# Second pair's input rows fetched with the late operands, and expert retrieval in seven pieces behind seven steps, in a hybrid decoder layer

## The chip, the cores and the metric

The kernel runs on one core of one Trainium2 chip. The metric is the device time of one execution in microseconds (us), all transfers from and to HBM included.

## The reference

One layer of a decoder runs over 512 prompt tokens and 8 x 4 sample tokens, width 1024, all in float32. First comes a mixer (projections, a causal convolution of width 31, dilated attention with 24 heads, gates, an output projection), then the part with which most of this text deals, a mixture of 16,384 one-neuron experts:

```python
def peer_block(hb):                                   # hb: normalised rows
    q = (hb @ w_peer_q).reshape(rows, 8, 2, 128)
    s = jnp.einsum('thpc,hpkc->thpk', q, sub_keys)    # two halves, 128 keys each
    s1, i1 = lax.top_k(s[:, :, 0], 16)
    s2, i2 = lax.top_k(s[:, :, 1], 16)
    cand = (s1[..., :, None] + s2[..., None, :]).reshape(rows, 8, 256)
    top_s, top_c = lax.top_k(cand, 16)
    idx = take(i1, top_c // 16) * 128 + take(i2, top_c % 16)
    g = softmax(top_s)
    a = jnp.einsum('td,tkd->tk', hb, expert_u[idx])
    return jnp.einsum('tk,tkd->td', g * gelu(a), expert_v[idx])
```

## The kernel before

**Tiles and pairs.** The prompt's four tiles of 128 rows are 0, 1, 2 and 3, the 32 sample rows are tile 4. `PAIRS` puts tiles 0, 1 and 4 through the mixer first and tiles 2 and 3 second. `plan()` writes the mixer out as 508 ticks of tasks; each engine's program walks the same ticks in order (`TICKS`), and semaphores alone join the engines. SP issues all plain transfers in this order, POOL the gathers.

**Steps.** The experts are worked off in 544 steps (`ST`). A step gathers 128 rows of 8 KB (one expert's `u` and `v` row for each partition, 1.05 MB) into one of the `RING` = 6 slots of the tile `ring` (POOL, L1106, an indirect transfer). DVE takes the dot product of the `u` half with the token's row in `rep` (L1945), ACT makes `gelu` and a folding matrix of it (L1514, L1518, L1521), PE adds the weighted `v` half up in `acc` (L1348) and counts `v_used`; with that count POOL may issue the gather that takes the slot next, six steps on. Steps 0 to 127 belong to tile 0, 128 to 255 to tile 1, 256 to 287 to tile 4, then 128 each to tiles 2 and 3. `MARK` says after which tick how many steps are done: 272 of them run among the ticks of the second pair's mixer, the last 272 alone behind it. The loop is the function `steps_upto` of each engine.

**Items.** Each tile has 8 heads, and each (tile, head) is an item of `ITEMS`: 40 in all. An item with 128 rows serves 16 steps, one of tile 4 serves 4. Its retrieval on DVE finds the 16 best of both halves of 128 scores, the 16 best of the 256 sums, and the experts' numbers and weights. `item_list` lets the retrieval of an item for 16 steps begin 16 steps before its first one; tile 4's items lie between these, at steps 8, 40, 72 and so on. `part(q, p)` is piece p of item q, and `PARTS` puts piece p behind the dot product of step at + p. Then PE spreads the result over the partitions (`spread`, L1310), DVE copies it to `pick` (`place`, L1903 and L1904), and POOL and ACT wait on `pick_ready` before the first step of the item. `place_picks` chooses the tick of spread and place, or in the last 272 steps the step at + 5 (`TAIL_PICKS`), where `place` comes two steps later on DVE. The first pair's scores go through HBM: SP fetches those of the next item (`load_scores`, at the step in `SCORES_AT`) when `half_done` says that the last one's halves are searched. ACT makes the exponentials (`head_exp`, L1503).

**Input rows.** `xt` holds two tiles of x in the tile `sx`, which the attention's scores use as well. The task `X0` of a tile waits on ACT for its rows (`x_in`), squares them (L1556), then POOL and DVE scale them and PE turns them (`XT`). For tiles 2 and 3 `X0` stands in the ticks of the first pair's query projection (`wq`), and SP fetches the rows in that same tick. `ENDS["late", 0]` is an earlier tick, at which the first pair's attention is over (`o_free`); there SP fetches operands of the first pair's end: x for the residual, norm weights, taps, sub keys (`skT`).

**Copies on the chip.** For tiles 2 and 3 the rows in `rep` are made on PE (`copy_rows`) and copied out by ACT.

Of the kernel before, what the change touches and what calls it, by code (L numbers as in the profile page):

```python
# [9 lines left out]
ALU = mybir.AluOpType  # L10
# [3 lines left out]
P = 128  # L14
# [18 lines left out]
LOW = -3.0e38  # L33
# [63 lines left out]
def tile_rows(t):  # L97
    return P if t < NT else SMP
# [104 lines left out]
LEAD_V, LEAD_A = 2, 2  # L203
# [244 lines left out]

ITEMS = item_list()
ITEM_NO = {(t, h): q for q, (_, t, h) in enumerate(ITEMS)}  # L450
PARTS = {}
for _q, (_at, _t, _h) in enumerate(ITEMS):
    for _p in range(4):
        if _at >= 0:
            PARTS.setdefault(_at + _p, []).append((_q, _p))
SCORES_AT = {ITEMS[q - 1][0] + 2 if q > 2 and (t, h) != (2, 0) else max(at - 3, 0): q for q, (at, t, h) in enumerate(ITEMS) if at >= 0}


def place_picks():

    tail = {}
    for q, (at, _, _) in enumerate(ITEMS):
        n = START if q == 0 else next((n for n in range(START, len(TICKS)) if MARK[n] + LEAD_V > at + 3), len(TICKS)) + 2
        if n < len(TICKS):
            TICKS[n].append(("P", q))
            TICKS[n].sort(key=lambda v: ORDER[v[0]])
        else:
            tail[at + 5] = q  # L470
    return tail


# [136 lines left out]
def program(nc, a, sc):  # L610
    with ExitStack() as ctx:
# [176 lines left out]
        def o_phase(p):  # L788
            return max(OB.no["O", x] for x in XS if PH_OF[pair(x)[0]] == p) + 1
# [29 lines left out]
        def _(eng):  # L819
# [110 lines left out]
            for n, tick in enumerate(TICKS):  # L930
# [7 lines left out]
                for p in range(2):  # L938
                    if n == ENDS["late", p]:
                        eng.wait_ge(o_free, o_phase(p))  # L940
                        for j in range(2):
                            eng.wait_ge(v_out[j], out_last(V_OUT, p, 2 + j))
                            if p == 0:
                                eng.wait_ge(hist_out[j], out_last(HIST, p, 2 + j))
                        for t in PAIRS[p][0:2]:
                            eng.dma_start(x1s[:, t % 2, :], a["x_prompt"][0, P * t:P * (t + 1), :]).then_inc(late_in, 16)
                        eng.dma_start(w2, a["norm2_w"].to_broadcast([P, D])).then_inc(late_in, 16)
                        if p == 0:
                            eng.dma_start(pt[:, D:D + 2 * P], a["taps"]).then_inc(taps_in, 16)
                            for j in range(2):  # L950
                                eng.wait_ge(ub_out[j], max(UB_OUT[i] for i, (t, _) in enumerate(GLU) if i % 2 == j and PH_OF[t] == 0))
                            for c in range(2):
                                load_last_u(c)
                        eng.dma_start(skT, a["sk_t"]).then_inc(late_in, 16)
                if n == ENDS["cp", NT, 1]:
                    eng.wait_ge(conv_v, DC * TAPS)
                    for c in range(QUAD):
                        row = slice(SUB * c, SUB * (c + 1))
                        eng.dma_start(x1d[row, :].rearrange("p (h x) -> p h x", h=2), xs.rearrange("t (h c x) -> t c h x", h=2, c=QUAD)[:, c]).then_inc(dlate_in, 16)
                        eng.dma_start(w2d[row, :].rearrange("p (h x) -> p h x", h=2),  # L960
                                      a["norm2_w"].rearrange("o (h c x) -> o c h x", h=2, c=QUAD)[:, c].to_broadcast([SUB, 2, P])).then_inc(dlate_in, 16)
                for v in tick:
                    if v[0] == "X0" and v[1] in (2, 3):
                        t = v[1]
                        eng.wait_ge(o_free, o_phase(0))
                        eng.dma_start(xt[:, t % 2, :], a["x_prompt"][0, P * t:P * (t + 1), :]).then_inc(x_in[t % 2], 16)
                    elif v[0] == "uo":
                        t, c = v[1:]
                        i = NTH["G", t, c]
                        freed(eng, ZB, z_free, ("glu", t, c))  # L970
# [528 lines left out]
        def _(eng):  # L1499
# [7 lines left out]
            def steps_upto(last):  # L1507
                for i in range(done[0], min(last, STEPS)):
                    t, h, j, s = ST[i]
                    if j == J_ORDER[t][0] and s == 0:  # L1510
                        eng.wait_ge(pick_ready, ITEM_NO[t, h] + 1)
                    if i >= 2:
                        eng.wait_ge(fold_ready, i - 1)
                    eng.activation(by_pick[:, i % 2, :], cst[:, C_FOLD:C_FOLD + SUB], ACT.Copy, scale=picks(i, 1)).then_inc(by_ready, 1)  # L1514
                    eng.wait_ge(dot_ready, i + 1)
                    if i >= 4:
                        eng.wait_ge(v_used, i - 3)
                    eng.activation(gel[:, i % 4:i % 4 + 1], dots[:, i % 4:i % 4 + 1], ACT.Gelu).then_inc(gel_ready, 1)  # L1518
                    eng.wait_ge(gel_ready, i + 1)
                    eng.wait_ge(by_ready, i + 1)  # L1520
                    eng.activation(fold[:, i % 4, :], by_pick[:, i % 2, :], ACT.Copy, scale=gel[:, i % 4:i % 4 + 1]).then_inc(fold_ready, 1)  # L1521
                    for n, u, k in MADE.get(i, ()):
                        eng.wait_ge(rep_made, n + 1)
                        eng.wait_ge(dot_ready, slot_before(u, k) + 1)
                        for w in range(2):
                            ins = eng.activation(rep[:, k, 512 * w:512 * (w + 1)], zb[w][:, :], ACT.Copy)
                        ins.then_inc(rep_ready, 1)
                    for q, p in PARTS.get(i, ()):
                        if p == 1:
                            head_exp(q)  # L1530
                done[0] = max(done[0], last)

# [263 lines left out]
        def _(eng):  # L1796
# [40 lines left out]
            def top16(values, index, x):  # L1837
                link(eng.max(values[:, 0:8], x))
                link(eng.max_index(index[:, 0:8], values[:, 0:8], x))  # L1839
                link(eng.match_replace(x, values[:, 0:8], x, LOW))  # L1840
                link(eng.max(values[:, 8:16], x))  # L1841
                return eng.max_index(index[:, 8:16], values[:, 8:16], x)  # L1842

            def halves(q):
                _, t, h = ITEMS[q]
                m, of = tile_rows(t), sco2
                if PH_OF[t]:
                    freed(eng, SB, s_free, ("SC", t, h // 2))
                    of = kept_scores(t)[:, 2 * KEYS * h:2 * KEYS * (h + 1)]
                elif q:  # L1850
                    eng.wait_ge(sco_in, 16 * q)
                else:
                    freed(eng, SB, s_free, ("SC", 0, 0))
                    link(eng.tensor_copy(sco2[:, :], sco[:, 0, 0:2 * KEYS]))
                for p in range(2):
                    ins = top16(tv[0:m, p, :], ti[0:m, p, :], of[0:m, KEYS * p:KEYS * (p + 1)])
                    if p:
                        signal(ins, half_done, q + 1)
                    else:
                        link(ins)  # L1860

            def candidates(q):
                m = tile_rows(ITEMS[q][1])
                link(eng.tensor_copy(tif[0:m, :, :], ti[0:m, :, :]))
                if q:
                    eng.wait_ge(o_ready, OB.no["P", q - 1] + 1)
                link(eng.tensor_tensor(cand[0:m, :, :], tv[0:m, 0, :].unsqueeze(2).to_broadcast([m, TOPK, TOPK]),
                                       tv[0:m, 1, :].unsqueeze(1).to_broadcast([m, TOPK, TOPK]), ALU.add))
                link(top16(cv[0:m, :], ci[0:m, :], cand[0:m, :, :].rearrange("p a b -> p (a b)")))
                signal(eng.tensor_scalar(nmx[0:m, :], cv[0:m, 0:1], -1.0, None, ALU.mult), top_ready, q + 1)  # L1870

            def keys_named(q, p):
                m = tile_rows(ITEMS[q][1])
# [8 lines left out]

            def experts(q):
                m = tile_rows(ITEMS[q][1])
                keys_named(q, 1)
# [19 lines left out]
                eng.sem_inc(o_free, 1)  # L1905

            def part(q, p):
                if p == 0:
                    halves(q)
                elif p == 1:  # L1910
                    candidates(q)
                elif p == 2:
                    keys_named(q, 0)
                else:
                    experts(q)

# [37 lines left out]
            for n, tick in enumerate(TICKS):  # L1954
# [182 lines left out]
                if n in CONV[0]:  # L2137
                    conv_upto(0, CONV[0][n])
                if START - 4 <= n < START:
                    part(0, n - START + 4)  # L2140
# [68 lines left out]
```

## Time and profile before

| | us |
|---|---|
| median of 3 runs | 2246.28 |
| lowest and highest run | 2244.76, 2247.51 |
| profiled execution, its own time | 2251.89 |
| span of the profiled execution | 2250.1 |
| DVE busy | 1469.5 (65%) |
| PE busy | 1631.4 (73%) |
| ACT busy, POOL busy | 867.5 (39%), 751.8 (33%) |
| bytes moved, mean rate | 745.18 MB, 331 GB/s |

The span runs from the first to the last instruction of the profiled execution, which took 5.61 us longer than the median of the three plain runs. All rows below are of that execution, so differences are worked out against 2251.89. A busy share is a mean over stages with different limits: up to about 530 us there are no expert steps, to about 1560 us steps and mixer run together, and behind that the steps run alone.

### The profile page before, as it was taken

To read this page: it belongs to the slowest core of one execution; us is meant where nothing else is said; L and a number is where in the kernel's file an instruction comes from. 1 tells how busy PE (TensorE), PEld (TensorE's weight loads), DVE (VectorE), ACT (ScalarE), POOL (GpSimd) and SP (SyncE) were. 2 spreads that over 40 slices of the span, in tenths; PEclk is the share of its full clock that TensorE was granted. 3 is DMA by queue.
4 is the path that set the end of the run, shared out by engine and by line. 5 is a ranking of instruction groups with operands and counts; after the bars stand their busy time and mean duration, and the time that the engine had idled before them with its cause. 6 is when DMAs were issued, how large, how long until landed. Compare 5 with 4: busy or idle time off the path is not lost.

```text
span 2250.1 us, 33792 instructions
## 1 busy us (share of the span) xinstructions
PE 1631.4 (73%) x11740; PEld 748.3 (33%) x11740; DVE 1469.5 (65%) x3591; ACT 867.5 (39%) x2442; POOL 751.8 (33%) x713
## 2 busy tenths in 40 slices
PE   7999999997898977777778989996444344444343
PEld 3556655443443433434343433342100001100000
DVE  2577764114658687878877767446766766766764
ACT  2122334012445434544546653334333333333332
POOL 1254200001332344333442323334444344344343
PEclk9999999998999989789888999997655556555555
DMA  5333556666898979899989999999999999999998
GB/s 192 130 110 110 200 217 237 251 201 259 324 400 339 378 302 374 303 374 364 383 332 381 362 397 405 380 406 401 389 387 412 411 406 408 389 404 399 391 386 354
DMA packets 125798, 745.18 MB, mean 331 GB/s; under 512 B 15892, under 2 KB 39052, under 8 KB 47916
## 3 DMA queue, kind: packets, MB, share of 16 engines
q0 software_dynamic: 78336, 570.46, 63.9%
q1 hardware_dynamic: 47292, 172.55, 20.6%
q8 instruction: 94, 1.54, 0.3%
q14 instruction: 76, 0.62, 0.1%
HBM read 727.36 MB, written 16.44 MB: 331 GB/s over the span
## 4 chain that ended last, share of the span: by engine, by line
PE 36%; DMA 25%; DVE 24%; issue 9%; ACT 4%; POOL 2%; SPq 0%; DVEq 0%; POOLq 0%; ACTq 0%
DMA ring<-in_expert_uv,pick 23%; PE z L1174 21%; DVE ring L1945 5%; PE acc L1348 5%; PE z L1180 2%; DMA sx<-in_x_prompt 1%; PE o L1209 1%; DVE ti L1839 1%; DVE ti L1842 1%; DVE cand L1880 1%; DVE e L1881 1%; DVE tv L1841 1%; DVE cand L1878 1%; DVE tmp L2016 1%; PE s L1478 1%
## 5 line engine op out<-in xcount | busy, mean ns | idle before, releaser
L1106 POOL DMA_INDIRECT ring<-in_expert_uv,pick x544 | 619.7, 1139 | 949.5 <-PE acc L1348 859.4
L1945 DVE CUSTOM_DVE_ANT_0 ring<-ring,rep 128x1024 f32<-128x1024 f32 x544 | 660.1, 1225 | 351.1 <-DMA ring<-in_expert_uv,pick 318.4
L1348 PE MATMUL acc<-ring,fold 128*32 128x256 f32 x4352 | 452.0, 506 | 456.0 <-ACT fold L1521 454.2
L1174 PE MATMUL z<-wts,hT 128*128 128x384 f32 (+1 forms) x1408 | 613.6, 573 | 7.6 <-ACT hT L1536 4.7
L1518 ACT ACTIVATE gel<-dots 128x1 f32<-128x1 f32 x544 | 109.9, 202 | 727.3 <-DVE dots L1945 723.6
L1348 PEld LDWEIGHTS acc<-ring,fold 128*32 128x32 f32 x4352 | 106.3, 124 | 767.2 <-ACT fold L1521 687.5
L1174 PEld LDWEIGHTS z<-wts,hT 128*128 128x128 f32 x1408 | 260.4, 199 | 259.8 <-issue 197.6
L1174 PE MATMUL z<-wts,yT 128*128 128x512 f32 x384 | 194.6, 643 | 10.9 <-ACT yT L1717 5.9
L1521 ACT ACTIVATE fold<-by_pick,gel 128x32 f32<-128x32 f32 x544 | 175.6, 323 | 18.0
L1514 ACT ACTIVATE by_pick<-cst,pick 128x32 f32<-128x32 f32 x544 | 168.1, 309 | 0.0
L1831 DVE SCALAR_TENSOR_TENSOR yT<-uT,vec,yT 128x256 f32<-128x256 f32 x240 | 107.8, 501 | 2.3
L1174 PEld LDWEIGHTS z<-wts,yT 128*128 128x128 f32 x384 | 71.5, 201 | 99.5 <-issue 99.4
L1071 POOL TENSOR_SCALAR xss<-xss 128x1 f32<-128x1 f32 (+1 forms) x10 | 2.0, 196 | 275.6 <-ACT kvr L1732 218.3
L1518 ACT ACT_TABLE_LOAD x70 | 89.8, 1283 | 1.2
L1071 POOL TENSOR_SCALAR ssq<-ssq 128x6 f32<-128x6 f32 (+1 forms) x40 | 21.6, 539 | 179.8 <-DVE ssq L2000 179.0
L1209 PE MATMUL o<-kvr,pt 128*128 128x64 f32 x432 | 59.1, 294 | 13.2 <-ACT pt L1536 10.3
L1402 PE MATMUL t<-cst,sx 128*128 128x128 f32 x216 | 39.6, 304 | 39.8 <-ACT hoT L1536 22.9
L1209 PEld LDWEIGHTS o<-kvr,pt 128*128 128x128 f32 x432 | 58.4, 211 | 23.8 <-ACT pt L1536 13.4
L2032 DVE SCALAR_TENSOR_TENSOR sx<-s,cst 128x512 f32<-128x512 f32 (+3 forms) x72 | 36.8, 552 | 39.6 <-PE s L1199 37.5
L1072 POOL TENSOR_TENSOR ssq<-ssq,half_m 128x6 f32<-128x6 f32 (+1 forms) x40 | 53.4, 1336 | 3.5 <-POOL ssq L1071 0.2
L1672 ACT ACTIVATE sx<-sx,nm 128x384 f32<-128x384 f32 (+3 forms) x32 | 32.5, 1017 | 56.6 <-DVE nm L2043 56.3
L1536 ACT ACTIVATE pt<-t 128x512 f32<-128x512 f32 (+2 forms) x64 | 33.6, 524 | 51.4 <-PE t L1402 51.3
(256 smaller groups left out, 1760.9 us busy)
## 6 DMA issues: line engine op xcount, KB each, us to landing
wts<-in_w_qkv SPq DMA_DIRECT2D x24, 1536.0 KB, 7.9
wts<-in_w_glu SPq DMA_DIRECT2D x8, 2048.0 KB, 9.8
wts<-in_w_gate SPq DMA_DIRECT2D x8, 2048.0 KB, 12.3
wts<-in_w_wq SPq DMA_DIRECT2D x8, 2048.0 KB, 10.7
ring<-in_k_cache SPq DMA_DIRECT2D x16, 768.0 KB, 7.3
ring<-in_v_cache SPq DMA_DIRECT2D x16, 768.0 KB, 7.0
ring<-in_expert_uv,pick POOLq DMA_INDIRECT x544, 10.8
wts<-in_w_cp SPq DMA_DIRECT2D x4, 2048.0 KB, 10.5
```

The costliest lines, as they stand in the source:

```text
L1072: return eng.tensor_tensor(to, to, half_m[0:m, 0:w], ALU.pow)
L1106: eng.indirect_dma_start(ring[:, i % RING, :], None, a["expert_uv"], bass.IndirectOffsetOnAxis(picks(i, 0).bitcast(U32), 0)).then_inc(row_ ...
L1174: mm = eng.matmul(bank[:, 0:w], of[:, k, :], rows[:, k, :], start=(k == 0), stop=(k == depth - 1))
L1180: mm = eng.matmul(to, of[:, k, :], by, start=(k == 0), stop=(k == depth - 1))
L1209: mm = eng.matmul(ob[:, 0:HD], pt[:, P * j:P * (j + 1)], vv[:, hp % 2, u, P * g + HD * w:P * g + HD * (w + 1)], start=(j == 0), stop=(j == ...
L1348: mm = eng.matmul(acc[b][SUB * c:SUB * (c + 1), col:col + 256], fold[:, i % 4, :], ring[:, i % RING, D + 256 * c:D + 256 * (c + 1)], start ...
L1402: mm = eng.transpose(tpb[:, P * (j - 4 * q):P * (j - 4 * q + 1)], s_sb[:, XN[x] % 2, P * j:P * (j + 1)], ident)
L1514: eng.activation(by_pick[:, i % 2, :], cst[:, C_FOLD:C_FOLD + SUB], ACT.Copy, scale=picks(i, 1)).then_inc(by_ready, 1)
L1518: eng.activation(gel[:, i % 4:i % 4 + 1], dots[:, i % 4:i % 4 + 1], ACT.Gelu).then_inc(gel_ready, 1)
L1521: eng.activation(fold[:, i % 4, :], by_pick[:, i % 2, :], ACT.Copy, scale=gel[:, i % 4:i % 4 + 1]).then_inc(fold_ready, 1)
L1831: ins = eng.scalar_tensor_tensor(out=out, in0=src, scalar=cw[:, c, tap:tap + 1], in1=out, op0=ALU.mult, op1=ALU.add)
L1945: eng.tensor_tensor_reduce(u, u, rep[:, j, :], 1.0, 0.0, ALU.mult, ALU.add, dots[:, i % 4:i % 4 + 1]).then_inc(dot_ready, 1)
```

## The change

It has two parts. SP fetches the rows of tiles 2 and 3 at the tick `ENDS["late", 0]`, as the last transfers of that group, and no longer at their `X0`. And the retrieval of an item is cut in seven pieces behind seven steps where it had four behind four: each half search alone, the sums with the first eight of their best, the second eight, each of the two key lookups alone, the experts' numbers. The operations are the same, and so is their order within an item. What hangs on the end of a retrieval moves along: `spread` and `place` come three steps later, `head_exp` is put behind step at + 4 where it was behind step at + 1, and the next item's scores are fetched one step later. Item 0's pieces stay in the same four ticks.

```diff
+PIECES = 7
 PARTS = {}
 for _q, (_at, _t, _h) in enumerate(ITEMS):
-    for _p in range(4):
+    for _p in range(PIECES):
         if _at >= 0:
             PARTS.setdefault(_at + _p, []).append((_q, _p))
-SCORES_AT = {ITEMS[q - 1][0] + 2 if q > 2 and (t, h) != (2, 0) else max(at - 3, 0): q for q, (at, t, h) in enumerate(ITEMS) if at >= 0}
+SCORES_AT = {ITEMS[q - 1][0] + 3 if q > 2 and (t, h) != (2, 0) else max(at - 3, 0): q for q, (at, t, h) in enumerate(ITEMS) if at >= 0}
...
-        n = START if q == 0 else next((n for n in range(START, len(TICKS)) if MARK[n] + LEAD_V > at + 3), len(TICKS)) + 2
+        n = START if q == 0 else next((n for n in range(START, len(TICKS)) if MARK[n] + LEAD_V > at + PIECES - 1), len(TICKS)) + 2
...
-            tail[at + 5] = q
+            tail[at + PIECES + 1] = q
...
                         eng.dma_start(skT, a["sk_t"]).then_inc(late_in, 16)
+                        if p == 0:
+                            for t in PAIRS[1]:
+                                eng.dma_start(xt[:, t % 2, :], a["x_prompt"][0, P * t:P * (t + 1), :]).then_inc(x_in[t % 2], 16)
...
-                    if v[0] == "X0" and v[1] in (2, 3):
-                        t = v[1]
-                        eng.wait_ge(o_free, o_phase(0))
-                        eng.dma_start(xt[:, t % 2, :], a["x_prompt"][0, P * t:P * (t + 1), :]).then_inc(x_in[t % 2], 16)
...
-                        if p == 1:
+                        if p == 4:
                             head_exp(q)
...
             def part(q, p):
-                if p == 0:
-                    halves(q)
-                elif p == 1:
-                    candidates(q)
-                elif p == 2:
-                    keys_named(q, 0)
+                if p < 2:
+                    half_search(q, p)
+                elif p < 4:
+                    candidates(q, p - 2)
+                elif p < 6:
+                    keys_named(q, p - 4)
                 else:
                     experts(q)
```

On SP the two fetches of x into `sx` stood directly behind a weight load that waits for PE (`z_ready`), in the ticks of the query projection, among the scores that go out to HBM (`x_sc`) and come back (`sco`):

```order
L827 DMA wts<-in_w_wq 128x4096 [waits z_ready]
L966 DMA sx<-in_x_prompt 128x1024 [waits o_free]
L1032 DMA x_sc<-tmp 128x512 [waits s_free_a]
L857 DMA sco<-x_sc 32x256 [waits sco_out0,half_done]
L1032 DMA x_sc<-tmp 32x512 [waits s_free_a]
L1032 DMA x_sc<-tmp 128x512 [waits s_free_a]
L827 DMA wts<-in_w_glu 128x4096 [waits z_ready]
L966 DMA sx<-in_x_prompt 128x1024 [waits o_free]
```

Now they stand as one group behind the sub keys (`kvr<-in_sk_t`), ahead of the next part of the sample tokens' value cache, which is read into the tile `ring` before the gathers use it:

```order
L849 DMA qTs<-x_uh 32x256 [waits ub_out1,ub_out0]
L849 DMA qTs<-x_uh 32x256
L955 DMA kvr<-in_sk_t 128x2048
L958 DMA sx<-in_x_prompt 128x1024 x2
L842 DMA ring<-in_v_cache 128x1536 [waits k_used]
L842 DMA ring<-in_v_cache 128x1536 x3
L828 DMA wts<-in_w_ap 128x2048 [waits z_ready]
```

Both fetches have moved past all weight loads of the output and query projections and past the first fetches of scores.

On DVE, behind the dot product (ISA; its line is 1945 before, 1957 in the changed kernel) of the first step of the last item, both half searches stood together, each of five operations, and the next step's dot product behind ten:

```order
L1945 ISA dots 128x1
L1838 MAX tv<-uT 128x8
L1839 MAX_INDEX ti<-tv,uT 128x8
L1840 MATCH_REPLACE uT<-tv,uT 128x128
L1841 MAX tv<-uT 128x8
L1842 MAX_INDEX ti<-tv,uT 128x8
L1838 MAX tv<-uT 128x8
L1839 MAX_INDEX ti<-tv,uT 128x8
L1840 MATCH_REPLACE uT<-tv,uT 128x128
L1841 MAX tv<-uT 128x8
L1842 MAX_INDEX ti<-tv,uT 128x8
L1945 ISA ring,dots<-ring,rep 128x1024
```

Now the next step's dot product stands behind five, and the second half behind that:

```order
L1957 ISA dots 128x1
L1838 MAX tv<-uT 128x8
L1839 MAX_INDEX ti<-tv,uT 128x8
L1840 MATCH_REPLACE uT<-tv,uT 128x128
L1841 MAX tv<-uT 128x8
L1842 MAX_INDEX ti<-tv,uT 128x8
L1957 ISA ring,dots<-ring,rep 128x1024
L1957 ISA dots 128x1
L1838 MAX tv<-uT 128x8
L1839 MAX_INDEX ti<-tv,uT 128x8
L1840 MATCH_REPLACE uT<-tv,uT 128x128
L1841 MAX tv<-uT 128x8
```

The second half search has moved behind one more dot product; the later pieces follow in the same way, one behind each of the next five.

## Rows read from the trace of the kernel before

**Rows 1.** The page's chain that ended last, by line.

```profile
DMA ring<-in_expert_uv,pick 23%; PE z L1174 21%; DVE ring L1945 5%; PE acc L1348 5%; PE z L1180 2%; DMA sx<-in_x_prompt 1%; PE o L1209 1%; DVE ti L1839 1%; DVE ti L1842 1%; DVE cand L1880 1%; DVE e L1881 1%; DVE tv L1841 1%; DVE cand L1878 1%; DVE tmp L2016 1%; PE s L1478 1%
```

**Rows 2.** By stage: busy us (instructions) of PE, PEld, DVE, ACT, POOL; PEclk, DMA share, GB/s.

```profile
500.00:620.00 120.00, 91.63 (x613) 47.19 (x615) 63.18 (x199) 43.30 (x121) 26.34 (x26) 0.89 0.79 290
...
900.00:1220.00 320.00, 244.05 (x1501) 126.59 (x1499) 267.37 (x695) 169.92 (x418) 120.10 (x106) 0.87 0.94 358
...
1600.00:2000.00 400.00, 171.55 (x1388) 38.60 (x1388) 283.71 (x708) 143.62 (x499) 179.26 (x154) 0.55 0.99 403
```

**Rows 3.** The chain, 480 to 660 us: start, length, what.

```profile
540.33 11.44 DMA sx<-in_x_prompt
...
581.16 14.90 DMA sx<-in_x_prompt
```

**Rows 4.** Waits, 500 to 620 us: total, times, longest.

```profile
ACT pt L1556 <- DMA sx<-in_x_prompt: 24.0, 2, 12.7
```

**Rows 5.** Timeline of PE, 520 to 612 us; in brackets the idle time before.

```profile
555.73 1.08 PE L1348 MATMUL acc<-ring,fold 128*32 128x256 f32 x8 [12.62 <-ACT fold L1521]
...
597.94 0.47 PE L1466 MATMUL t<-cst,uT 128*128 128x128 f32 x1 [10.30 <-ACT hoT L1536]
```

**Rows 6.** Timeline of SP's issues, 380 to 640 us.

```profile
415.62 2.26 SPq L841 DMA_DIRECT2D ring<-in_v_cache  x4
```

**Rows 7.** The chain, 380 to 460 us.

```profile
416.96 9.46 DMA ring<-in_v_cache
```

**Rows 8.** Timeline of DVE, 2033 to 2052 us.

```profile
2034.04 1.22 DVE L1945 CUSTOM_DVE_ANT_0 ring<-ring,rep 128x1024 f32<-128x1024 f32 x1 [1.25 <-DMA ring<-in_expert_uv,pick]
...
2037.03 0.29 DVE L1838 MAX8 tv<-uT 128x8 f32<-128x128 f32 x1
...
2038.87 1.22 DVE L1945 CUSTOM_DVE_ANT_0 ring<-ring,rep 128x1024 f32<-128x1024 f32 x1
...
2041.69 0.09 DVE L1840 MATCH_VALUE_LOAD cand<-cv,cand 128x8 f32 x1
...
2043.39 1.22 DVE L1945 CUSTOM_DVE_ANT_0 ring<-ring,rep 128x1024 f32<-128x1024 f32 x1
...
2046.54 1.23 DVE L1945 CUSTOM_DVE_ANT_0 ring<-ring,rep 128x1024 f32<-128x1024 f32 x1
...
2049.05 0.17 DVE L1886 SCALAR_TENSOR_TENSOR e<-e 128x16 f32<-128x16 f32 x1
...
2050.09 1.23 DVE L1945 CUSTOM_DVE_ANT_0 ring<-ring,rep 128x1024 f32<-128x1024 f32 x1
...
2051.24 1.22 DVE L1945 CUSTOM_DVE_ANT_0 ring<-ring,rep 128x1024 f32<-128x1024 f32 x1
```

**Rows 9.** Busy time in stretches of 2 us.

```profile
2044.00:2046.00 2.00, 0.07 (x4) 0.07 (x8) 1.86 (x7) 1.94 (x5) 0.00 (x0) 0.50 1.01 422
...
2048.00:2050.00 2.00, 1.08 (x8) 0.20 (x8) 1.79 (x7) 0.55 (x3) 0.77 (x2) 0.50 0.64 160
```

**Rows 10.** Timeline of POOL's gather issues, 2036 to 2062 us.

```profile
2042.13 0.94 POOL L1106 DMA_INDIRECT ring<-in_expert_uv,pick  x1 [3.90 <-PE acc L1348]
...
2047.31 1.26 POOL L1106 DMA_INDIRECT ring<-in_expert_uv,pick  x1 [4.24 <-PE acc L1348]
```

**Rows 11.** The chain, 2034 to 2064 us.

```profile
2051.36 0.21 ACT gel L1518
...
2051.97 1.12 PE acc L1348 x8
```

**Rows 12.** Timeline of DVE: the dot products of steps 272, 528 and 540.

```profile
1528.10 1.23 DVE L1945 CUSTOM_DVE_ANT_0 ring<-ring,rep 128x1024 f32<-128x1024 f32 x1 [1.26 <-DMA ring<-in_expert_uv,pick]
...
2204.18 1.23 DVE L1945 CUSTOM_DVE_ANT_0 ring<-ring,rep 128x1024 f32<-128x1024 f32 x1 [1.25 <-DMA ring<-in_expert_uv,pick]
...
2234.35 1.23 DVE L1945 CUSTOM_DVE_ANT_0 ring<-ring,rep 128x1024 f32<-128x1024 f32 x1 [1.25 <-DMA ring<-in_expert_uv,pick]
```

**Rows 13.** Waits, whole span.

```profile
DVE pick L1903 <- PE o L1310: 29.7, 11, 7.3
```

More of the change, by code:

```diff
@@ L962, in _ @@
                 for v in tick:
-                    if v[0] == "X0" and v[1] in (2, 3):
-                        t = v[1]
-                        eng.wait_ge(o_free, o_phase(0))
-                        eng.dma_start(xt[:, t % 2, :], a["x_prompt"][0, P * t:P * (t + 1), :]).then_inc(x_in[t % 2], 16)
-                    elif v[0] == "uo":
+                    if v[0] == "uo":
                         t, c = v[1:]
@@ L1842, in top16, with scores_of @@
                 return eng.max_index(index[:, 8:16], values[:, 8:16], x)
-            def halves(q):
+            def scores_of(q, p):
                 _, t, h = ITEMS[q]
                 m, of = tile_rows(t), sco2
+                if p:
+                    return m, kept_scores(t)[:, 2 * KEYS * h:2 * KEYS * (h + 1)] if PH_OF[t] else of
                 if PH_OF[t]:
@@ L1854, in halves, with half_search, candidates @@
                     link(eng.tensor_copy(sco2[:, :], sco[:, 0, 0:2 * KEYS]))
[L1855 to L1862, printed above, removed]
-                m = tile_rows(ITEMS[q][1])
+                return m, of
+            def half_search(q, p):
+                m, of = scores_of(q, p)
+                ins = top16(tv[0:m, p, :], ti[0:m, p, :], of[0:m, KEYS * p:KEYS * (p + 1)])
+                if p:
+                    signal(ins, half_done, q + 1)
+                else:
+                    link(ins)
+            def candidates(q, p):
+                m = tile_rows(ITEMS[q][1])
+                flat = cand[0:m, :, :].rearrange("p a b -> p (a b)")
+                if p:
+                    link(eng.match_replace(flat, cv[0:m, 0:8], flat, LOW))
+                    link(eng.max(cv[0:m, 8:16], flat))
+                    link(eng.max_index(ci[0:m, 8:16], cv[0:m, 8:16], flat))
+                    signal(eng.tensor_scalar(nmx[0:m, :], cv[0:m, 0:1], -1.0, None, ALU.mult), top_ready, q + 1)
+                    return
                 link(eng.tensor_copy(tif[0:m, :, :], ti[0:m, :, :]))
@@ L1868, in candidates @@
                                        tv[0:m, 1, :].unsqueeze(1).to_broadcast([m, TOPK, TOPK]), ALU.add))
-                link(top16(cv[0:m, :], ci[0:m, :], cand[0:m, :, :].rearrange("p a b -> p (a b)")))
-                signal(eng.tensor_scalar(nmx[0:m, :], cv[0:m, 0:1], -1.0, None, ALU.mult), top_ready, q + 1)
+                link(eng.max(cv[0:m, 0:8], flat))
+                link(eng.max_index(ci[0:m, 0:8], cv[0:m, 0:8], flat))
             def keys_named(q, p):
@@ L1884, in experts @@
                 m = tile_rows(ITEMS[q][1])
-                keys_named(q, 1)
                 link(eng.scalar_tensor_tensor(out=e12[0:m, 0, :], in0=e12[0:m, 0, :], scalar=float(KEYS), in1=e12[0:m, 1, :], op0=ALU.mult, op1=ALU.add))
@@ L2139, in _ @@
                 if START - 4 <= n < START:
-                    part(0, n - START + 4)
+                    k = 2 * (n - START + 4)
+                    for p in range(k, min(k + 2, PIECES)):
+                        part(0, p)
                 steps_upto(lead(n, LEAD_V))
```

## The prediction

> **What bounds the kernel now.** I read the page's chain first: the kernel has no single bound. Of the work that ended last, 23% is gathers of expert rows, 21% the mixer's matrix products, and 1% is a transfer of x [rows 1]. So I went by stages. In the stage from 900 to 1220 us DVE is busy 267 of 320 us, PE 244, and the transfer engines 94%: three engines near their limit that wait for one another. From 1600 to 2000 us only expert steps run, PE is busy 43%, DVE 71% and the transfer engines 99%, with 403 GB/s [rows 2]. There the gathers are the bound, and the question is whether they run without holes.
>
> The fetch of x is seen in the chain: 11.44 us from 540.33 and 14.90 us from 581.16 [rows 3]. ACT stands still for them 24.0 us in two waits [rows 4], and PE behind ACT twice, 12.62 us before 555.73 and 10.30 us before 597.94 [rows 5].
>
> The retrieval is seen in DVE's timeline of one item near 2034 us [rows 8]. Dot products start at 2034.04, 2038.87, 2043.39, 2046.54 and 2050.09, and the next at 2051.24, so that one with nothing behind it takes 1.15 us. Without retrieval the last period's steps 528 to 540 go from 2204.18 to 2234.35, 2.514 us a step [rows 12]; this is the pace of the gathers. The four pieces make 16.05 us of four steps that were due in 10.06: DVE ends 6.0 us late.
>
> What the lateness does is seen two steps on. A gather takes the slot that a step six before it gives free. The dot product of 2038.87 is 2.32 us late against the pace; the gather it releases goes out at 2042.13, and between 2044 and 2046 us the transfers still run at 422 GB/s. The dot product of 2043.39 is 4.32 us late; its gather goes out at 2047.31, and between 2048 and 2050 the rate is 160 GB/s [rows 9, 10]. So a lateness of 2.3 us is covered by the queue, one of 4.3 us is not.
>
> **The tail: 272 steps alone.** Step 272 starts at 1528.10 and step 528 at 2204.18 [rows 12]: 676.08 us for 256 steps, 2.641 us a step or 42.25 us for 16. At 2.514 it would be 40.22. The difference is 2.03 us an item, and 16 items are searched there (at steps 272 to 512, every 16): 32.5 us.
>
> Would seven pieces close the holes? The pieces come out of [rows 8]: a half search 1.84 us (2035.19, which is 2034.04 and 1.15, to 2037.03, and again to 2038.87), the sums with the first eight 1.67 (2040.02 to 2041.69), the second eight 1.70, the first lookup 2.00, the second 1.36, the experts' numbers 1.04; in all 11.45. A step takes 1.15 and its piece. Against 2.514 DVE's lateness then goes 0.48, 0.95, 1.26, 1.59, 2.23, 2.23, 1.90 us and falls off by 1.36 a step. Its peak of 2.23 lies just below the 2.32 that left no hole. I take the whole 32 us. Above it, with every step at the 422 GB/s of [rows 9], a step takes 2.485 us and the gain is 16 x 16 x 0.156 = 40 us; below, it is nothing, if the holes have another cause (a rival).
>
> ACT's exponential moves three steps later and its waits on DVE with it. Its operations are the same and it is needed only by the last piece, two steps on; I count 0.
>
> **The input rows.** Both fetches go out with the sub keys, before 415.62 us, where SP issues the next part of the value cache [rows 6], over 120 us before ACT wants them. ACT's waits vanish. PE loses 22.9 us in its two stalls, of which I leave 2 for work of ACT that still lies between (in the first stall PE resumes 3.96 us after the rows have landed at 551.77). So 21. But the transfers of this stage must then go into a shorter time: 290 GB/s over 120 us [rows 2] are 34.8 MB; less 1.05 MB of x they need 341 GB/s over 99 us. That is below 403 and so can be done, yet gathers and weights will now and then stand in each other's way; I give 4 us back (bounds 0 and 10). At their new place the fetches are 1.05 MB ahead of the value cache, which is on the chain with 9.46 us [rows 7]: 2.6 us at 403 GB/s if the queue is full then, 0 if it has run dry; I take 2, since the transfers ahead of it were issued in one group. Net 15 us, between 10 and 23.
>
> The rows show why x was slow: 0.52 MB took 11.44 and 14.90 us [rows 3], though at 403 GB/s they need 1.3; they went out right behind a weight load. The Trainium skill (DMA: Bandwidth & Descriptors, Issuing engines are not separate DMA queues) says that transfers from all issuing engines run on the same 16 engines and interleave; the trace agrees. By that rule the early fetch gets nothing for free and pays the upper bound at the value cache, which would make the sum smaller by 0.6 us.
>
> **The middle: 272 steps among the second pair's ticks.** 23 items are searched there. DVE does ticks and pieces in one line, so a long piece holds up mixer tasks on which PE waits, and the ring has holes as in the tail. If each item gave 2.03 us as in the tail, this were 47 us; if PE and the order of the ticks set the pace alone, 0. As three engines share the bound [rows 2], I take a quarter, 12 us, an estimate.
>
> The waits that are moved: `place` stands three steps later, at + 10. POOL may issue the gather of step at + 16 when PE has counted step at + 10. PE's products for a step end 1.85 us behind its dot product (2051.24 to 2053.09) [rows 8, 11], and `place` is two small copies, at most 0.74 us by the mean 0.37 of the five operations of a half search. So the picks come about 1.1 us before they can be used, where they came three steps before. Cost 0 here; what is queued behind a late `place` is all of DVE and POOL's gathers (a rival). SP fetches scores one step later; the next item begins at least 5 steps on, some 12 us or more even at the tail's pace. Cost 0.
>
> **Sum.** 32 + 15 + 12 = 59. The profiled execution took 2251.89 us and would take 2193. The median of the runs is 5.61 us below the profiled execution, so I predict 2187.
>
> **The rivals.**
>
> The gathers keep their mean pace whatever DVE does: the holes are made up by the bursts behind them, and 42.25 us for 16 is what memory gives. For it: at 403 GB/s the tail is near its best short stretches. Against it: 160 GB/s right where a gather was late [rows 9, 10], and 2.514 us over 12 steps without an item. Then tail and middle give nothing and x alone gives 15: 2231. The Trainium skill (DMA: Bandwidth & Descriptors, Specifications) gives about 358 GB/s as the limit of HBM for a core. By it a step could not be under 2.93 us and the tail would have nothing to give; the trace disagrees, with 403 over 400 us and 422 in a short stretch [rows 2, 9].
>
> The time that x gives is lost again: the gathers and weights behind 540 us take as long as before, and the stall comes back as a wait of DVE on the ring. For it: the stage's transfer engines are busy 79% with the stalls in it. Against it: 341 GB/s are below what the tail moves. Then the gain is 44: 2202.
>
> Slower: `place` becomes the thing that gathers wait for. DVE waits there for PE's `spread`, 29.7 us in 11 of the 40 places now, at most 7.3 [rows 13], and the margin shrinks from three steps to 1.1 us. If `place` is late by w on the other 39 items, this costs 39 x (w - 1.1); from w = 2.6 us the gain of 59 is gone. At 4 us each it costs 113: 2300. Against it: PE spreads two steps ahead of `place`, and the searches end four steps ahead.
>
> The change does not act: DVE is late by as much in the end (the same 11.45 us), ACT or the ticks set the pace: 2246.
>
> **How the numbers follow.** Forecast 0.63; mean pace kept 0.18; x lost again 0.10; `place` late 0.06; no effect 0.03. The likeliest is 2187. With the upper bounds of tail and x and 30 for the middle the gain is 93: 2153. Upwards the range takes in the second rival and goes halfway into the first's, to 2226, which leaves out about 2 in 10. The likeliest case's own range is 2153 to 2205. A measurement of this kernel tells some 0.2% (4.5 us) from no change. Faster 0.91, within 0.2% 0.03, slower 0.06.
>
> **What would show it.** Tail: 16 steps in 40 to 40.5 us, no 2 us stretch below 300 GB/s behind an item, dot products of an item some 3 us apart. Input rows: no wait of ACT on x behind 500 us, and PE without the two stalls; the value cache's piece of the chain up to 2 us longer. Middle: step 272 some 27 us earlier than 1528. I am wrong if holes stay though DVE is less than 2.5 us late, or if POOL waits for `pick`.

## The result, and the profile after

The changed kernel takes 2190.74 us, the median of 4 runs (2186.95 to 2192.8); the kernel before, on the same chip, 2245.52 (4 runs, 2237.85 to 2247.51). The ratio is 0.9754 with an interval of 0.9737 to 0.9771. The forecast was 2187. The profiled execution took 2191.63 us with a span of 2189.8.

The page's chain that ended last, by line, which answers to [rows 1]:

```profile
DMA ring<-in_expert_uv,pick 25%; PE z L1174 20%; DVE ring L1957 9%; PE acc L1348 4%; PE z L1180 2%; PE o L1209 1%; DVE ti L1839 1%; DVE tmp L2028 1%; DVE ti L1842 1%; DVE nm L2054 1%; DVE tmp L2021 1%; POOL ring L1106 1%; PE s L1199 1%; ACT fold L1521 1%; DVE tv L1841 1%
```

The transfer of x is gone from it. Gathers (25%) and dot products (9%, before 5%) hold more of a shorter time.

By stage, columns as in [rows 2]:

```profile
500.00:620.00 120.00, 111.48 (x782) 57.55 (x781) 71.42 (x218) 54.06 (x151) 32.53 (x34) 0.97 0.92 351
900.00:1220.00 320.00, 256.35 (x1577) 130.19 (x1574) 265.88 (x675) 181.69 (x443) 128.37 (x110) 0.88 0.96 371
1600.00:2000.00 400.00, 179.87 (x1444) 39.95 (x1444) 294.55 (x733) 149.65 (x522) 206.70 (x159) 0.53 1.01 418
```

Between 500 and 620 us PE is busy 111 us instead of 92, and the transfers run at 351 GB/s instead of 290. In the tail they run at 418 instead of 403. In the middle DVE is busy as long as before, and 1577 matrix products fit where 1501 did.

DVE's timeline of one item in the tail, dot products alone, which answers to [rows 8], and those of steps 272 and 528, which answer to [rows 12]:

```profile
1495.04 1.23 DVE L1957 CUSTOM_DVE_ANT_0 ring<-ring,rep 128x1024 f32<-128x1024 f32 x1 [1.26 <-DMA ring<-in_expert_uv,pick]
...
1983.42 1.23 DVE L1957 CUSTOM_DVE_ANT_0 ring<-ring,rep 128x1024 f32<-128x1024 f32 x1 [1.25 <-DMA ring<-in_expert_uv,pick]
1986.41 1.23 DVE L1957 CUSTOM_DVE_ANT_0 ring<-ring,rep 128x1024 f32<-128x1024 f32 x1
1989.39 1.23 DVE L1957 CUSTOM_DVE_ANT_0 ring<-ring,rep 128x1024 f32<-128x1024 f32 x1
...
1995.06 1.23 DVE L1957 CUSTOM_DVE_ANT_0 ring<-ring,rep 128x1024 f32<-128x1024 f32 x1
1998.21 1.23 DVE L1957 CUSTOM_DVE_ANT_0 ring<-ring,rep 128x1024 f32<-128x1024 f32 x1
...
2004.08 1.22 DVE L1957 CUSTOM_DVE_ANT_0 ring<-ring,rep 128x1024 f32<-128x1024 f32 x1
...
2145.16 1.23 DVE L1957 CUSTOM_DVE_ANT_0 ring<-ring,rep 128x1024 f32<-128x1024 f32 x1 [1.25 <-DMA ring<-in_expert_uv,pick]
```

The starts of an item's steps now stand 2.8 to 3.2 us apart instead of up to 4.8. From 1495.04 to 2145.16 are 650.1 us for 256 steps, 40.63 us for 16 (before 42.25).

POOL's gathers behind that item, and the transfers in stretches of 2 us at the same place; the views are those of [rows 10] and [rows 9]:

```profile
1989.67 1.76 POOL L1106 DMA_INDIRECT ring<-in_expert_uv,pick  x1 [1.23 <-PE acc L1348]
...
1998.32 1.93 POOL L1106 DMA_INDIRECT ring<-in_expert_uv,pick  x1 [1.23 <-PE acc L1348]
2002.11 0.94 POOL L1106 DMA_INDIRECT ring<-in_expert_uv,pick  x1 [1.86 <-PE acc L1348]
```

```profile
1996.00:1998.00 2.00, 1.06 (x8) 0.20 (x8) 1.83 (x8) 1.62 (x3) 1.10 (x1) 0.50 1.01 422
1998.00:2000.00 2.00, 0.02 (x3) 0.00 (x0) 1.93 (x5) 1.97 (x5) 1.68 (x1) 0.50 1.02 422
2000.00:2002.00 2.00, 1.08 (x8) 0.20 (x8) 1.93 (x5) 0.85 (x4) 0.25 (x1) 0.50 1.01 401
2002.00:2004.00 2.00, 1.08 (x8) 0.20 (x8) 1.86 (x5) 0.74 (x3) 0.94 (x2) 0.50 1.01 410
```

The gathers still go out unevenly (3.79 us from 1998.32 to 2002.11), but the rate stays at 401 and above where it fell to 160 before.

At the start the value cache holds the mixer up for longer than in [rows 7]. The chain of the changed kernel, and then PE's timeline there:

```profile
416.92 11.56 DMA ring<-in_v_cache
```

```profile
428.61 5.92 PE L1262 MATMUL o<-ring,rep 128*32 128x512 f32 x32 [4.26 <-DMA ring<-in_v_cache]
...
549.33 0.64 PE L1348 MATMUL acc<-ring,fold 128*32 128x256 f32 x8 [1.96 <-ACT fold L1521]
```

The transfer takes 2.1 us more than the 9.46 before. The 32 products behind it begin at 428.61 (before 426.56) and take 5.92 us (before 3.64). The last line is the place of the stall of 12.62 us in [rows 5]: 1.96 are left. Nothing answers to the second stall, or to ACT's wait on x in [rows 4].

### The profile page after: what moved, and what is told of

It is laid out like the page before. It is cut to its first block, busy times and chain, and to the rows that moved or that the text cites. A ratio compares the mean times of both kernels' runs of the same rounds, so it can differ in the third digit from the quotient of the medians.

```text
span 2189.8 us, 33814 instructions
## 1 busy us (share of the span) xinstructions
PE 1623.5 (74%) x11740; PEld 742.6 (34%) x11740; DVE 1466.1 (67%) x3591; ACT 865.0 (40%) x2442; POOL 796.4 (36%) x713
## 4 chain that ended last, share of the span: by engine, by line
PE 35%; DMA 26%; DVE 25%; issue 8%; ACT 5%; POOL 2%; SPq 0%; DVEq 0%; ACTq 0%; POOLq 0%
DMA ring<-in_expert_uv,pick 25%; PE z L1174 20%; DVE ring L1957 9%; PE acc L1348 4%; PE z L1180 2%; PE o L1209 1%; DVE ti L1839 1%; DVE tmp L2028 1%; DVE ti L1842 1%; DVE nm L2054 1%; DVE tmp L2021 1%; POOL ring L1106 1%; PE s L1199 1%; ACT fold L1521 1%; DVE tv L1841 1%
## 5 line engine op out<-in xcount | busy, mean ns | idle before, releaser
L1106 POOL DMA_INDIRECT ring<-in_expert_uv,pick x544 | 665.4, 1223 | 876.5 <-PE acc L1348 804.9
L1174 PE MATMUL z<-wts,yT 128*128 128x512 f32 x384 | 188.1, 625 | 13.2 <-ACT yT L1717 8.6
L1672 ACT ACTIVATE sx<-sx,nm 128x384 f32<-128x384 f32 (+3 forms) x32 | 32.5, 1016 | 51.5 <-DVE nm L2055 51.2
## 6 DMA issues: line engine op xcount, KB each, us to landing
ring<-in_expert_uv,pick POOLq DMA_INDIRECT x544, 11.3
```

The lines of the kernel that those rows point to most:

```text
L1106: eng.indirect_dma_start(ring[:, i % RING, :], None, a["expert_uv"], bass.IndirectOffsetOnAxis(picks(i, 0).bitcast(U32), 0)).then_inc(row_ ...
L1174: mm = eng.matmul(bank[:, 0:w], of[:, k, :], rows[:, k, :], start=(k == 0), stop=(k == depth - 1))
```

## The experiments

All runs in one table, from the trace of one execution each: the starts of the dot products of steps 0, 16, 272 and 528, and us for 16 steps in the middle (16 to 272) and in the tail (272 to 528). The last column is the median of the plain times; "(one)" marks a single run.

```
              step 0  step 16 step 272 step 528  middle  tail   median of times
before         531.0   607.9   1528.1   2204.2   57.51  42.26   2245.52
after          535.3   594.6   1495.0   2145.2   56.28  40.63   2190.74
after_again    536.6   593.4   1495.6   2145.6   56.39  40.62   2190.37
after_third    534.4   594.1   1493.7   2143.8   56.23  40.63   2189.45
x_only         534.1   592.4   1507.8   2178.6   57.21  41.92   2226.57
pieces_only    534.8   617.0   1514.1   2164.5   56.07  40.65   2210.05
tail_pieces    535.8   595.8   1512.8   2162.4   57.31  40.60   2207.48
x_behind       531.2   589.7   1489.6   2141.4   56.25  40.73   2188.87
x_sk_behind    530.5   588.0   1484.8   2135.1   56.05  40.65   2184.76
x_sk_second    530.9   589.0   1485.5   2134.7   56.03  40.58   2181.98
spaced4        535.9   592.9   1499.6   2152.0   56.67  40.78   2200.22
late_place     536.6   592.9   1493.2   2143.6   56.27  40.65   2190.18 (one)
ring5_after    536.8   595.7   1537.8   2208.9   58.88  41.94   2255.36 (one)
ring5_before   532.5   611.8   1581.5   2288.8   60.61  44.21   2335.47 (one)
```

### Each half of the change alone: x_only, pieces_only, tail_pieces, after_again

The theory is the forecast's: tail, input rows and middle are three gains of their own. The first rival says that the gathers keep their mean pace and only x counts; the second, that x's time is lost again behind 540 us.

x_only is the kernel before, with the early fetch alone:

```diff
                         eng.dma_start(skT, a["sk_t"]).then_inc(late_in, 16)
+                        if p == 0:
+                            for t in PAIRS[1]:
+                                eng.dma_start(xt[:, t % 2, :], ...).then_inc(x_in[t % 2], 16)
...
-                    if v[0] == "X0" and v[1] in (2, 3):
-                        t = v[1]
-                        eng.wait_ge(o_free, o_phase(0))
-                        eng.dma_start(xt[:, t % 2, :], ...).then_inc(x_in[t % 2], 16)
-                    elif v[0] == "uo":
+                    if v[0] == "uo":
```

> Early fetch of x alone, retrieval in four pieces as before. My theory: the two ACT waits on x go and PE's stalls with them, less some 4 us because the value cache lands later; step 16 starts near 595 us and the median is 13 us below before, near 2232 us. Rival, that the stage's transfers take the time back: within 4 us of before, 2242 to 2250 us.

pieces_only is the changed kernel with this diff turned round, so that x comes late as before.

> Seven pieces alone, x fetched late as before. My theory: the tail gains 26 us (40.6 us for 16 steps), the middle some 17, so near 2203 us, and the gains of this and of the early fetch alone add up to the 55 us of both. Rival, that the gathers keep their mean pace: tail at 42.2 us for 16 steps and a median above 2235 us.

tail_pieces has the early fetch, and seven steps for a retrieval only where it starts at step 272 or behind; the earlier items are done behind four steps, in the groups of before:

```diff
+def behind(q):
+    return (0, 1, 2, 3, 4, 5, 6) if ITEMS[q][0] >= BASE[2] - LAG else (0, 0, 1, 1, 2, 3, 3)
...
-            PARTS.setdefault(_at + _p, []).append((_q, _p))
+            PARTS.setdefault(_at + behind(_q)[_p], []).append((_q, _p))
...
-            tail[at + PIECES + 1] = q
+            tail[at + behind(q)[-1] + 2] = q
```

For those earlier items ACT's exponential goes back to the step behind `at`, and the next item's scores are fetched one step earlier again, for all items.

> Early x, seven pieces in the last 272 steps alone, four pieces for the items before. My theory, that tail and middle gain each by itself: tail at 40.6 us for 16 steps, 17 us slower than the changed kernel, near 2207 us. Rival, that pieces help in the tail alone and the earlier step 272 is due to x: as the changed kernel, 2191 us.

after_again is the changed kernel on this chip.

> The changed kernel once more, beside the others on the same chip: 2187 to 2193 us by every theory.

Measured, with the kernel before at 2243.89 on this chip: x_only 2226.57 (ratio 0.9922, 0.9896 to 0.9948), pieces_only 2210.05 (0.9846, 0.9823 to 0.9869), tail_pieces 2207.48 (0.9832, 0.9806 to 0.9859), after_again 2190.37 (0.9756, 0.9733 to 0.978). The halves add: 17.3 and 33.8 are 51.2, and both together give 53.5. So x's time isn't lost again, and the pieces act without it. tail_pieces has the tail of the changed kernel (40.60) and the middle of x_only (57.31 against 57.21). It ends 17.1 us above after_again: that is the middle's share. x_only in turn ends 19.1 us above tail_pieces: that is the tail's. So by the medians the change consists of 17.3 us for x, 19.1 for the tail and 17.1 for the middle.

x_only did better than its forecast of 2232; pieces_only missed its own, near 2203, by 7 us. Its tail is the expected 40.65 and its middle 56.07, but step 16 comes 9.1 us later than in the trace of the kernel before. There ACT waits 28.8 us for x instead of 24.0; why x comes still later in this kernel isn't shown.

What the middle's share consists of is seen in the waits between 610 and 1490 us (total, times, longest). In tail_pieces:

```profile
DVE ring L1968 <- DMA ring<-in_expert_uv,pick: 117.6, 71, 7.4
POOL ssq L1083 <- DVE ssq L2023: 82.4, 16, 11.6
```

and in after_again:

```profile
DVE ring L1957 <- DMA ring<-in_expert_uv,pick: 110.7, 64, 6.2
POOL ssq L1071 <- DVE ssq L2012: 72.7, 16, 8.7
```

DVE waits 6.9 us less for gathers, and POOL 9.7 us less for DVE's sums of squares, a part of the mixer's norms. That both grow shorter fits the reason of the forecast (a long piece leaves holes in the ring and holds up the mixer's tasks). How the 17 us divide between the two isn't settled by it: waits of two engines may overlap.

### Where x goes out: x_behind, x_sk_behind, x_sk_second, after_third

After the first runs the value cache at the start was the one place where the change lost time. x_behind sends x behind the small operands that SP fetches after the value cache's last part, instead of ahead of it:

```diff
-                        if p == 0:
-                            for t in PAIRS[1]:
-                                eng.dma_start(xt[:, t % 2, :], ...).then_inc(x_in[t % 2], 16)
...
                                       ....to_broadcast([SUB, 2, P])).then_inc(dlate_in, 16)
+                    for t in PAIRS[1]:
+                        eng.dma_start(xt[:, t % 2, :], ...).then_inc(x_in[t % 2], 16)
```

> The changed kernel with x for tiles 2 and 3 fetched behind the sample's late operands, that is behind the value cache's second part, near 424 us. My theory: the value cache lands after 9.5 us again, PE's pause ahead of it is short and its clock stays up, step 0 starts at 531 us where it started at 535, and the median is 4 us below the changed kernel, near 2187 us. Rival, that the steps' transfers set the pace from 540 us on and hide the start: 2191 us.

x_sk_behind moves the sub keys of the first pair there too:

```diff
-                        eng.dma_start(skT, a["sk_t"]).then_inc(late_in, 16)
+                        if p:
+                            eng.dma_start(skT, a["sk_t"]).then_inc(late_in, 16)
...
+                    eng.dma_start(skT, a["sk_t"]).then_inc(late_in, 16)
                     for t in PAIRS[1]:
```

> As the one before, and the sub keys (1 MB) fetched there too. My theory: the value cache lands 2.6 us earlier still (1.05 MB at 403 GB/s), so about 6.5 us below the changed kernel, near 2184 us. Rival, as before: 2191 us.

Measured, with the kernel before at 2246.0: x_behind 2188.87 (0.9738, 0.9722 to 0.9754) and x_sk_behind 2184.76 (0.9727, 0.9708 to 0.9747). In both, step 0 stands where it stood in the kernel before. x_behind's median doesn't decide between 2187 and the rival's 2191, since the changed kernel didn't run beside it. The 2.6 us that the sub keys were to bring weren't there: the value cache lands at 425.7 us in x_sk_behind and at 426.7 in x_behind, and the times of the two overlap (2181.22 to 2190.58, 2185.06 to 2190.61). To set the better one beside the changed kernel itself, both ran once more on one chip (kernel before 2245.29), as x_sk_second and after_third.

> The changed kernel, the measure for the run beside it on the same chip: 2187 to 2193 us.

> x and the sub keys both fetched behind the value cache, once more and beside the changed kernel. My theory: step 0 near 531 us where the changed kernel has 535 to 537, and 4 to 7 us below it in time. Rival, that the gain seen was scatter between chips: within 2 us of it.

x_sk_second took 2181.98 (2181.22 to 2188.22; 0.9722, 0.9701 to 0.9743), after_third 2189.45 (2185.9 to 2195.23; 0.9747, 0.9724 to 0.977). The medians are 7.5 us apart, and the intervals of the ratios overlap. PE's timeline of x_sk_second shows where a part of the time comes from:

```profile
425.95 3.64 PE L1263 MATMUL o<-ring,rep 128*32 128x512 f32 x32 [1.47 <-DMA ring<-in_v_cache]
```

The products begin 2.7 us earlier than in the first profile of the changed kernel, and take 3.64 us instead of 5.92. Beside after_third, step 0 comes 3.5 us earlier, step 16 5.0, step 272 8.2 and step 528 9.1; what it gains behind step 16 has no cause that these runs show, and may be the scatter of single executions. This is the best version found.

### How much lateness the queue covers: spaced4, late_place, ring5_after, ring5_before

The forecast says that not the length of a piece matters but how late DVE is in sum against the pace of the gathers, and that the queue covers 2.3 us and not 4.3. spaced4 tells the two apart. The four long pieces are back, but each with an idle step behind it, so that an item still takes seven steps:

```diff
+def behind(q):
+    return (0, 0, 2, 2, 4, 6, 6)
```

with the uses of `behind` as in tail_pieces, and `place` where the changed kernel has it.

> The changed kernel with the four long pieces back, but behind every second step (at, + 2, + 4, + 6); place stands as in the changed kernel. By the lateness at 2.514 us a step: 2.3, 1.0, 3.0, 1.6, 2.2, 0.9, 1.9 us, a peak of 3.0. My theory, that the sum of lateness decides: between the 2.3 that left no hole and the 4.3 that did, 0 to 0.7 us an item, 2191 to 2202 us. Rival, that the length of one piece (3.7 us) decides: the tail at 42 us for 16 steps again, 2213 us or more.

Measured: 2200.22 (0.9793, 0.9772 to 0.9814). The tail takes 40.78 for 16 steps, near the changed kernel's 40.63 and far from 42.26. From the traces, the mean of 16 items: us from each of the first nine steps to the next.

```
before     4.83 4.54 3.15 3.54 1.22 1.15 1.15 1.80 1.85
after      3.02 2.99 2.82 2.85 3.23 2.52 2.18 1.19 1.93
spaced4    4.83 1.15 4.52 1.15 3.22 1.15 3.60 1.19 1.83
```

Against a pace of 2.486 (the steps behind 528 of the changed kernel's trace), the greatest lateness in sum is 6.1 us before, 2.5 after, and 3.0 in spaced4 (4.83, 1.15 and 4.52 less three times 2.486). A piece of 3.7 us does little harm if a short step stands behind it. The exponential stands three steps later in spaced4 and in the changed kernel than before; it isn't what held the tail up, since between 1600 and 2000 us DVE waits for ACT in none of the three traces. The middle gains less than with seven pieces (56.67 against 56.28).

late_place puts `place` of the tail's items two steps later, against the rival that this copy becomes the thing that gathers wait for:

```diff
-            tail[at + PIECES + 1] = q
+            tail[at + PIECES + 3] = q
```

> The changed kernel with spread and place two steps later in the last 272 steps, at + 10 and + 12. The picks then come two steps or 5.0 us behind where they stand, 3.9 us behind the release of the slot that they serve. If the margin of 1.1 us is all there is: 16 x 3.9 us, 62 us slower, 2253 us. If the queue covers a late gather up to some 2.3 to 3 us: 1 to 1.6 us an item, 16 to 26 us slower, 2207 to 2217 us. If picks have slack of two steps: 2191 us.

One execution took 2190.18, with the kernel before at 2248.82. The time is that of the third case, but the picks had no slack. The waits of late_place between 1600 and 2000 us:

```profile
POOL ring L1106 <- DVE pick L1916: 42.3, 10, 4.7
```

POOL did wait for the picks, at ten items, 4.2 us each, and from the gather ahead of an item's first one to that first one it is 5.6 us instead of 2.6 (means of the items from step 304 on). Yet the tail takes 40.65 us for 16 steps. So the mechanism is that of the second case, a queue that covers a late gather, with more cover than I gave it: 3 us cost nothing. The gathers queued ahead cover the delay, and POOL sends the next ones quickly (1.2, 1.7 and 1.3 us apart in the mean).

ring5_after and ring5_before use five of the ring's six slots, in the kernel after and in the one before. Fewer slots cover less lateness, so the pace should fall where DVE is late, and more where it is later.

```diff
-RING = 6
+RING = 5
```

> The changed kernel with 5 ring slots in use where there were 6, so the queue of gathers is 2.5 us shorter. My theory, that the queue covers the lateness: the pace without retrieval stays near 2.5 us a step, but the 2.2 us of lateness now make a hole, 0.4 to 2.2 us an item, so 41 to 42.5 us for 16 steps in the tail and 2200 to 2235 us in all. Rival, that the lateness of DVE has nothing to do with the queue: 40.6 us for 16 steps and 2191 us.

> The kernel before with 5 ring slots in use. My theory: every hole grows by the 2.5 us that the queue is shorter, 44.8 us for 16 steps in the tail, 40 us there and more in the middle, 2290 us or above. Rival, that the holes are the memory's own: 42.2 us for 16 steps, 2246 us.

One execution each, on the same chip: 2255.36 and 2335.47. The stretch from 1600 to 2000 us of ring5_after:

```profile
1600.00:2000.00 400.00, 180.37 (x1438) 41.39 (x1438) 283.63 (x697) 144.38 (x508) 201.04 (x154) 0.54 1.00 405
```

and of ring5_before:

```profile
1600.00:2000.00 400.00, 173.12 (x1426) 40.81 (x1417) 272.30 (x674) 142.08 (x492) 168.63 (x146) 0.57 0.95 381
```

The transfers fall from 418 to 405 GB/s in the one and from 403 to 381 in the other. Steps without an item behind them keep 2.486 us in both. So it's the lateness that costs, not the ring by itself: 1.3 us an item after (41.94 against 40.63) and 2.0 before (44.21 against 42.26). The tails were forecast at 41 to 42.5 and at 44.8, ring5_before in all at 2290 or above. I had expected ring5_after between 2200 and 2235 in all; I had left out that the middle loses too, 2.6 us for 16 steps (58.88 against 56.28), some 42 us over its 256 steps.

## Why the prediction was right

By places, from the two profiled executions: up to step 16 the changed kernel gains 13.3 us, in the middle 19.7, in the tail 26.0, behind it 1.2; together 60.2. The forecast's sum was 59, with 15 for the input rows, 12 for the middle and 32 for the tail. The medians are 54.8 apart, and by the medians of the halves the three shares are, in the same order, 17, 17 and 19. The mechanisms held, but all three sizes were off: the tail was put too high, the other two too low, and they made up for one another. That the sum came within 4 us of the median is in part luck.

**The tail: 26 instead of 32 by the profiles, 19 by the medians.** The holes are closed: of 302 stretches of 2 us between steps 288 and 528 none is below 300 GB/s, where before 18 of 316 were. The greatest lateness was forecast as 2.23 us and is 2.5, and what the queue covers lies where the forecast had it, at 2.3 or more: 3.0 us cost next to nothing (spaced4). Two sizes in the term were off. The first is the tail of the kernel before, 42.25 us for 16 steps, which is that of one execution, 5.61 us above the median. x_only has the same four pieces there and takes 41.92, so about 5 us of the 32 are most likely that execution's own and not the pieces'; against x_only the tail gains 20.6 us. The second is the pace that is left. I took 40.22 us for 16 steps, from a stretch without items; it is 40.63, outside the 40 to 40.5 that I gave as a sign. Sixteen gathers are 16.78 MB, by the page's row of the gathers' queue (MB of all 544):

```profile
q0 software_dynamic: 78336, 570.46, 64.6%
```

In 40.63 us that is 413 GB/s. All transfers together make 418 in this stretch, so the others take 5 of them, or about 0.5 us of 16 steps, and they aren't there behind step 528, the kind of stretch that the pace came from. In the changed kernel's own stretch there 16 steps take 39.78 us (2.486 a step), so some 0.35 us stay open. Ring and pieces have little more to give here: 418 stands near the 422 of [rows 9]. The Trainium skill (Perfetto Trace Analysis, Roofline) puts a core that runs alone at up to about 435 GB/s, the limit of its 16 transfer engines; the trace, with 418 over 400 us, agrees.

**The input rows: 13 instead of 15 by the profiles, 17 by the medians.** From step 0 to step 16 the time falls by 17.6 us (76.9 to 59.3), where 21 less 4 given back were forecast. The term that was off is the value cache: 2 were forecast, bounds 0 and 2.6, and step 0 comes 4.2 later. The transfer itself takes 2.1 of it. The rest goes with TensorE's clock, which the forecast left out. PE pauses 4.26 us instead of 2.19 and the products behind the pause take 2.3 us longer. In a window's row the granted clock is the number behind the busy times of the five engines; in the changed kernel:

```profile
424.00:426.00 2.00, 0.35 (x1) 0.00 (x0) 0.69 (x1) 0.00 (x0) 0.00 (x0) 1.00 1.02 421
426.00:428.00 2.00, 0.00 (x0) 0.00 (x0) 0.00 (x0) 0.00 (x0) 0.00 (x0) 0.61 1.03 426
428.00:430.00 2.00, 1.39 (x8) 0.46 (x12) 0.00 (x0) 0.00 (x0) 0.00 (x0) 0.50 1.07 305
430.00:432.00 2.00, 2.00 (x13) 0.45 (x8) 0.00 (x0) 0.00 (x0) 0.00 (x0) 0.50 0.36 57
```

and in the kernel before:

```profile
426.00:428.00 2.00, 1.44 (x16) 0.65 (x20) 0.00 (x0) 0.00 (x0) 0.00 (x0) 1.00 1.05 366
428.00:430.00 2.00, 2.00 (x24) 0.48 (x13) 0.00 (x0) 0.00 (x0) 0.00 (x0) 1.00 0.46 68
```

The clock goes from 1.00 to 0.50 (2.4 to 1.2 GHz) in the pause and stays there for most of the products. x_behind, which takes away the transfer ahead of the value cache, has a pause of 1.77 us, products of 3.64, and step 0 at 531.2: both parts go together. pieces_only, without an early fetch, is late too: a pause of 3.12 us, products of 5.02, and step 0 at 534.8. There the value cache's last part went out late, at 419.59 us, behind an issue on SP that took 2.19 us, and then landed in 8.64. In the eight traces with x ahead of it that part takes 11.3 to 11.8 us to land and step 0 stands at 534.1 to 536.8; in the other five without, it takes 8.1 to 9.5 and step 0 stands at 530.5 to 532.5. So x ahead of the value cache costs step 0 about 4.5 us in the mean.

By the medians x gains 17 us (x_only), not 13: how much of that comes behind step 16 isn't settled by single traces.

**The middle: 20 instead of 12 by the profiles, 17 by the medians.** The estimate of a quarter (of 47 us) should have been somewhat over a third, by tail_pieces. That three engines near their limit share the bound fits: by the medians an item gives 0.74 us there (17.1 by 23) and 1.2 in the tail (19.1 by 16), where the gathers alone are the bound. With the early rows and the middle together step 272 comes 33 us earlier, where I gave 27 as a sign.

**The waits that were costed at nothing.** DVE's wait for `spread` is 15.5 us in 10 places, at most 5.0, less than in [rows 13], over the whole span:

```profile
POOL ring L1106 <- DVE pick L1916: 25.7, 1, 25.7
DVE pick L1915 <- PE o L1310: 15.5, 10, 5.0
```

POOL's one wait for `pick`, the sign of being wrong, stands ahead of the first gather of all and was 25.7 us before as well. So the margin of 1.1 us was enough. But the price in that rival was wrong: in late_place picks some 3 us too late cost nothing in the tail, since the queue of gathers takes them up as it does DVE's lateness.

**The rivals.** The mean pace did not stay (tail 40.63, and 40.65 in pieces_only). x's time was not lost again (x_only). `place` was not late to any effect. The change acts.

## What to carry to other kernels

Where a ring of transfers runs at the memory's pace, what counts is how late the engine that frees the slots is in sum, not how long one piece of its other work is: cut or space that work so that the sum stays below what the queue has been measured to cover (here, with six slots of 2.5 us, a sum that rose to 3.0 us cost nearly nothing, and one that rose past 4.3 to 6.1 left holes; what lies between wasn't tried). An early fetch is put behind the transfers for which a busy engine waits, not simply as early as possible; here this brought step 0 back to where it stood before. A change that makes TensorE wait 2 us longer may cost as much again by the clock, as it did here. And the loss read from one trace is checked against a second kernel with the same code in that place: here about 5 of 32 us seem to belong to the one execution that had been profiled.

## What was not expected of the hardware

The products behind the value cache have two durations, and they go with the pause ahead of them. From the traces, PE's pause and the duration of the same 32 products, in us:

```
x_sk_behind 1.46 3.64     pieces_only 3.12 5.02     after       4.26 5.92
x_sk_second 1.47 3.64     late_place  4.00 6.50     ring5_after 4.33 6.23
ring5_before 1.59 3.64    after_again 4.06 6.41     tail_pieces 4.46 6.08
x_behind    1.77 3.64     spaced4     4.16 6.35
before      2.19 3.64     x_only      4.24 5.34     after_third 4.30 5.34
```

Five runs keep 3.64 us; the other nine take 5.0 to 6.5, and not in the order of their pauses. The Trainium skill (TensorE: Matmul & The Clock Gate, What's actually happening) says that a gate sets the clock by how busy the engine has been of late. The granted clock of 0.50 in the rows above agrees.
